# The expert loop of a two-layer block: nine weight places in turn, rows gathered with the selection stationary, and the last turns of the gated units moved

## What is computed

```python
logits = h @ w_router + b_router
topv, idx = lax.top_k(logits, 4)          # of 32 experts
gates = softmax(topv)
# the tokens of an expert, in blocks:
gu = xblk @ w_gate_up[e] + b_gate_up[e]    # 1024 -> 2048
gate = minimum(gu[:, :1024], 7.0); up = clip(gu[:, 1024:], -7.0, 7.0)
act = (up + 1.0) * (gate * sigmoid(1.702 * gate))
y = act @ w_down[e] + b_down[e]            # 1024 -> 1024
out[token] += y * gate_of_token
```

## Time and profile before

| | |
|---|---|
| median of 3 runs | 2026.39 us (2024.31 to 2032.32) |
| the profiled execution | 2024.82 us, of which the span of instructions is 2023.0 us |
| TensorE busy | 1954.4 us (97%), 10632 products |
| VectorE, ScalarE, GpSimd busy | 920.9 us (46%), 534.1 us (26%), 79.8 us (4%) |
| mean granted TensorE clock | 0.992 |
| moved by DMA | 560.29 MB, mean 277 GB/s |
| chain that ended last | PE 64%, DMA 21% (the weights of the experts 20%), DVE 7%, ACT 3% |

### The profile page before, as it was taken

The page is one execution under the profiler, slowest core; times in us unless marked ns, Lnnn a source line. Parts: engine busy times, 40 slices in busy tenths (PEclk is TensorE's granted clock), DMA queues, the critical chain, the costliest instruction groups (busy, mean ns, idle before and its releaser), DMA issues.

```text
span 2023.0 us, 26217 instructions
## 1 busy us (share of the span) xinstructions
PE 1954.4 (97%) x10632; PEld 1235.7 (61%) x10632; DVE 920.9 (46%) x1615; ACT 534.1 (26%) x792; POOL 79.8 (4%) x115
## 2 busy tenths in 40 slices
PE   7989999999999999999999999999999999999998
PEld 5767787444444444344344434687788887878886
DVE  5664556333223332332233233366666545556544
ACT  3444352011011101110010111222434434555432
POOL 1210000000000000000000000010320000000000
PEclk9999999999999999999999999999999999999999
DMA  6342228889999999999999999542326464445452
GB/s 248 137 160 84 94 103 314 365 367 429 427 428 428 428 428 428 428 428 428 427 428 427 429 427 429 212 150 100 105 85 228 151 214 166 158 145 205 170 195 76
DMA packets 106456, 560.29 MB, mean 277 GB/s; under 512 B 5904, under 2 KB 11280, under 8 KB 81808
## 3 DMA queue, kind: packets, MB, share of 16 engines
q1 hardware_dynamic: 102528, 551.61, 67.9%
q10 hardware_dynamic: 3856, 7.67, 1.2%
HBM read 558.21 MB, written 1.05 MB: 276 GB/s over the span
## 4 chain that ended last, share of the span: by engine, by line
PE 64%; DMA 21%; DVE 7%; ACT 3%; issue 2%; POOL 2%; SPq 0%; ACTq 0%; POOLq 0%; DVEq 0%
DMA ring<-in_w_gate_up_dram 20%; PE ps L1101 14%; PE ps L827 9%; PE ps L828 9%; PE ps L829 9%; PE ps L1125 6%; PE ps L1067 3%; PE ps L1200 3%; PE ps L1055 2%; DVE split_w L1997 2%; PE ps L1208 1%; PE ps L887 1%; POOL small L768 1%; PE ps L1325 1%; DMA gains<-in_gains_dram 1%
## 5 line engine op out<-in xcount | busy, mean ns | idle before, releaser
L1101 PE MATMUL ps<-ring,arena 128*64 128x512 f32 x2000 | 440.5, 595 | 8.8 <-DMA ring<-in_w_gate_up_dram 8.8
L1101 PEld LDWEIGHTS ps<-ring,arena 128*64 128x64 f32 x2000 | 139.5, 137 | 294.0 <-issue 269.8
L2373 DVE TENSOR_SCALAR arena<-ps 128x512 f32<-128x512 f32 x32 | 22.1, 692 | 504.6 <-PE ps L1101 504.6
L1956 DVE TENSOR_TENSOR split_w<-ring,split_w 128x1024 fp32r<-128x1024 f32 (+2 forms) x176 | 203.9, 1205 | 77.0 <-ACT split_w L1750 76.5
L1125 PE MATMUL ps<-ring,arena 128*64 128x512 f32 x1024 | 226.8, 595 | 0.0
L827 PE MATMUL ps<-split_w,act_parts 128*128 128x512 f32 (+1 forms) x544 | 209.8, 386 | 2.0 <-issue 1.0
L829 PE MATMUL ps<-split_w,act_parts 128*128 128x512 f32 (+1 forms) x544 | 205.6, 378 | 0.0
L828 PE MATMUL ps<-split_w,act_parts 128*128 128x512 f32 (+1 forms) x544 | 205.3, 377 | 0.0
L1750 ACT ACTIVATE split_w<-ring 128x1024 fp32r<-128x1024 f32 (+2 forms) x176 | 171.7, 1033 | 107.3 <-PE ps L829 107.3
L1125 PEld LDWEIGHTS ps<-ring,arena 128*64 128x64 f32 x1024 | 70.7, 137 | 133.3 <-issue 133.3
L1067 PEld LDWEIGHTS ps<-actT,arena 128*128 128x128 f32 x1056 | 129.9, 200 | 27.5 <-issue 27.5
(11 more groups left out here) (333 smaller groups left out, 2382.2 us busy)
## 6 DMA issues: line engine op xcount, KB each, us to landing
ring<-in_w_gate_up_dram SPq DMA_DIRECT2D x125, 2048.0 KB, 21.9
ring<-in_w_down_dram SPq DMA_DIRECT2D x64, 2048.0 KB, 19.7
ring<-in_f_w_dram SPq DMA_DIRECT2D x28, 2048.0 KB, 8.0
ring<-in_w_in_dram SPq DMA_DIRECT2D x14, 2048.0 KB, 8.0
ring<-in_a_w_in_dram SPq DMA_DIRECT2D x8, 2048.0 KB, 7.9
ring<-in_b_w_qkv_dram SPq DMA_DIRECT2D x6, 2048.0 KB, 7.8
arena<-in_w_gate_up_dram SPq DMA_DIRECT2D x3, 2048.0 KB, 14.0
ring<-in_f_w_dram SPq DMA_DIRECT2D x4, 1536.0 KB, 6.9
```

The costliest lines, as they stand in the source:

```text
L1101: mm = pe.matmul(ps[half, bank, :], xeT[:, 2 * c + j, :], w[:, j, col:col + 512], start=False, stop=(c == 3 and j == 1), skip_group_check= ...
L1956: dve.tensor_tensor(part_place(load, 1, k, n)[:, s_, :], raw_place(load, k, n)[:, s_, :], part_place(load, 0, k, n)[:, s_, :], ALU.subtract)\
L2373: dve.tensor_scalar(gate_c, ps[:, 1, :], 7.0, None, ALU.min).then_inc(m_gate, 1)
```

## The change

Of the expert loop: (1) the six ring places, in the order `RING_ORDER`, and the three extra ones form nine places. In the first 15 blocks (`GROUPED`, written out in groups of three blocks) chunk c of block b goes to place (6b + c) mod 9; from block 15 on the six ring places are used as before. (2) The gather has the selection stationary and the tokens moving: four products of 512 columns, two tiles by two halves of the columns, which land in the lower and the upper 64 partitions of bank 0. The rows are then not turned: ScalarE copies bank 0 to `xe_rows`, four turns of TensorE follow, and VectorE evacuates them as before. (3) The activation's turns go to bank 2, VectorE copies the activation before the rows, and ScalarE copies the rows behind the Silu. (4) The fill of `weightsT` goes from VectorE to GpSimd. Of the gated units: turns 10 and 11 stand in the middle of piece 1's products, one for each tile.

The diff, cut to its core (the renaming of semaphores and unchanged lines are left out):

```diff
@@ -335,20 +335,16 @@
 
 
 EXTRA = 3
-FIRST_SLOTS = (4, 5, 2, 1, 0, 3)
-FIRST_ORDER = (3, 4, 0, 1, 2, 5)
-
-
-def slot_of(b, chunk):
-
-    if b == 0:
-        return FIRST_SLOTS[chunk]
-    return FIRST_SLOTS[(chunk + EXTRA) % RING]
-
-
-def loads_of(b, chunk):
-
-    return loads_before(slot_of(b, chunk)) + (1 if b == 0 or chunk >= EXTRA else 0)
+PLACES = RING + EXTRA
+RING_ORDER = (1, 0, 4, 5, 2, 3)
+GROUP = 3
+GROUPED = 15
+MINBLK = S * TOPK // BLK
+
+
+def place_of(j, chunk):
+
+    return (RING * j + chunk) % PLACES
 
 
 def loads_before(slot):
...
@@ -517,7 +515,9 @@
             return ap
 
         extra = [arena[:, 5120 + SLOT * i:5120 + SLOT * (i + 1)] for i in range(EXTRA)]
+        places = [ring[:, s, :] for s in RING_ORDER] + extra
         h2n = area(0, NT, D)
+        xe_rows = rows[:, 1280:1792]
         gate_c, up_c, sig, act_e = area(2048, 512), area(2560, 512), area(3072, 512), area(17408, 512)
         act_eT, y_e, xeT = area(3584, 4, P), area(4096, 512), area(4608, KD, BLK)
         match, matchw = spot(0, NT * TOPK, BLK), spot(512, NT * TOPK, BLK)
...
@@ -679,36 +679,42 @@
 
                 return w_gu[e, c] if c < 4 else w_dn[e, c - 4]
 
-            def expert_chunk(b, e, c):
-                s = slot_of(b, c)
-                sync.dma_start(ring[:, s, :], expert_weights(e, c)).then_inc(loaded[s], 16)
-
-            for i, c in enumerate(FIRST_ORDER):
-                if i < 2:
-                    sync.wait_ge(pre_split, quarters_done(OUT_LOAD + i, 3))
+            def expert_chunk(place, e, c):
+                sync.dma_start(places[place], expert_weights(e, c)).then_inc(place_in[place], 16)
+
+            def grouped_block(b, j, e):
+
+                for c in range(RING):
+                    if c >= EXTRA:
+                        sync.wait_ge(used[c - EXTRA], b)
+                    elif place_of(j, c) < RING:
+                        sync.wait_ge(used[c + EXTRA], b - 1)
+                    expert_chunk(place_of(j, c), e, c)
+
+            for c in range(RING):
+                if c < 2:
+                    sync.wait_ge(pre_split, quarters_done(OUT_LOAD + c, 3))
                 else:
-                    sync.wait_ge(gemm_ready, G_OUT + i // 2 * 2)
-                expert_chunk(0, 0, c)
+                    sync.wait_ge(gemm_ready, G_OUT + c // 2 * 2)
+                expert_chunk(c, 0, c)
             sync.wait_ge(r_table, 1)
-            blocks = sync.value_load(tab[0:1, 48:49], min_val=TOPK, max_val=MAXBLK)
-            second_e = sync.value_load(tab[0:1, 1:2], min_val=0, max_val=NE - 1)
-            for c in range(EXTRA):
-                sync.dma_start(extra[c], expert_weights(second_e, c)).then_inc(extra_in[c], 16)
-            for c in range(EXTRA, RING):
-                sync.wait_ge(used[c - EXTRA], 1)
-                expert_chunk(1, second_e, c)
-            third_e = sync.value_load(tab[0:1, 2:3], min_val=0, max_val=NE - 1)
-            for c in range(RING):
-                if c < EXTRA:
-                    sync.wait_ge(used[c + EXTRA], 1)
-                else:
-                    sync.wait_ge(used[c], 2)
-                expert_chunk(2, third_e, c)
-            with sync.Fori(3, blocks) as b:
+            blocks = sync.value_load(tab[0:1, 48:49], min_val=MINBLK, max_val=MAXBLK)
+            for b in range(1, GROUP):
+                grouped_block(b, b, sync.value_load(tab[0:1, b:b + 1], min_val=0, max_val=NE - 1))
+            with sync.Fori(GROUP, GROUPED, GROUP) as first:
+                for j in range(GROUP):
+                    e = sync.value_load(tab[0:1, bass.ds(first + j, 1)], min_val=0, max_val=NE - 1)
+                    for c in range(RING):
+                        if c < EXTRA:
+                            sync.wait_ge(used[c + EXTRA], first + (j - 1))
+                        else:
+                            sync.wait_ge(used[c - EXTRA], first + j)
+                        expert_chunk(place_of(j, c), e, c)
+            with sync.Fori(GROUPED, blocks) as b:
                 e = sync.value_load(tab[0:1, bass.ds(b, 1)], min_val=0, max_val=NE - 1)
                 for c in range(RING):
                     sync.wait_ge(used[c], b)
-                    expert_chunk(2, e, c)
+                    expert_chunk(c, e, c)
 
             gdn_out, moba_in, moba_out = (t[n][0].rearrange("(k p) n -> p k n", p=P) for n in
                                           ("a_w_out_2", "b_w_qkv_2", "b_w_out_2"))
...
@@ -777,6 +783,8 @@
                     m += 1
             row_scales(2)
             row_scales(3)
+            pool.wait_ge(r_logits, 2)
+            pool.memset(weightsT, 0.0).then_inc(m_gtsb, 1)
 
             def power(c, n, mult, add, done):
 
...
@@ -1062,28 +1070,43 @@
             def gather(n):
 
                 pe.wait_ge(m_s, n)
-                for k in range(KD):
-                    for tile in range(NT):
-                        mm = pe.matmul(ps[:, 0, k * BLK:(k + 1) * BLK], h2n_c[:, tile, k // 2, k % 2, :],
-                                       sel[:, tile, :], start=(tile == 0), stop=(tile == 1),
-                                       skip_group_check=True)
+                for tile in range(NT):
+                    for h, half in enumerate((low, high)):
+                        mm = pe.matmul(ps[half, 0, :].rearrange("p (c j q) -> p c j q", c=2, j=2),
+                                       sel[:, tile, :],
+                                       h2n_c[:, tile, 2 * h:2 * h + 2], start=(tile == 0),
+                                       stop=(tile == 1), skip_group_check=True)
                 mm.then_inc(m_gathered, 1)
 
+            def turn_rows(n):
+
+                pe.wait_ge(m_row_copy, n)
+                for i in range(4):
+                    mm = pe.transpose(ps[:, 0, i * P:(i + 1) * P], xe_rows[:, i * P:(i + 1) * P],
+                                      ident)
+                mm.then_inc(m_gathered, 1)
+
             pe.wait_ge(r_table, 1)
-            blocks = pe.value_load(tab[0:1, 48:49], min_val=TOPK, max_val=MAXBLK)
+            blocks = pe.value_load(tab[0:1, 48:49], min_val=MINBLK, max_val=MAXBLK)
             gather(1)
+            turn_rows(1)
             pe.wait_ge(bias_split, 1)
 
-            def weights_in(b, at, c):
-
-                if at == 1 and c < EXTRA:
-                    pe.wait_ge(extra_in[c], 16)
-                    return extra[c]
-                s = slot_of(at, c)
-                pe.wait_ge(loaded[s], 16 * b + 16 * loads_of(at, c))
-                return ring[:, s, :]
-
-            def expert_block(b, at):
+            def grouped_weights(g, j, c):
+
+                place = place_of(j, c)
+                lap = (RING * j + c) // PLACES
+                laps = lap + 1 + (loads_before(RING_ORDER[place]) if place < RING else 0)
+                pe.wait_ge(place_in[place], 32 * g + 16 * laps)
+                return places[place]
+
+            def late_weights(b, c):
+
+                laps = loads_before(RING_ORDER[c]) + 2 * GROUPED // GROUP - GROUPED + 1
+                pe.wait_ge(place_in[c], 16 * b + 16 * laps)
+                return places[c]
+
+            def expert_block(b, weights_in):
 
                 pe.wait_ge(m_hot, b + 1)
                 pe.wait_ge(m_gtsb, b + 1)
...
@@ -1093,7 +1116,7 @@
                           skip_group_check=True).then_inc(m_biased, 1)
                 pe.wait_ge(m_xe, b + 1)
                 for c in range(4):
-                    w = weights_in(b, at, c).rearrange("p (j n) -> p j n", n=2 * FF)
+                    w = weights_in(c).rearrange("p (j n) -> p j n", n=2 * FF)
                     for j in range(2):
                         for bank in (1, 2):
...
@@ -1106,11 +1129,11 @@
                 pe.wait_ge(m_y, b + 1)
                 combine((0,))
                 pe.wait_ge(m_act, b + 1)
-                pe.wait_ge(m_xe, b + 2)
                 act_4 = act_e.rearrange("p (q j) -> p j q", j=4)
                 for j in range(4):
-                    mm = pe.transpose(ps[:, 0, j * P:(j + 1) * P], act_4[:, j, :], ident)
+                    mm = pe.transpose(ps[:, 2, j * P:(j + 1) * P], act_4[:, j, :], ident)
                 mm.then_inc(m_turned, 1)
+                turn_rows(b + 2)
                 combine((1,))
                 pe.wait_ge(m_dup, b + 1)
                 for tile in range(NT):
...
@@ -1127,10 +1150,11 @@
                                            w[:, j, n * 512:(n + 1) * 512], start=(c == 4 and j == 0),
                                            stop=(c == 5 and j == 3), skip_group_check=True)
                     mm.then_inc(used[c], 1)
-            for at in range(2):
-                expert_block(at, at)
-            with pe.Fori(2, blocks) as b:
-                expert_block(b, 2)
+            with pe.Fori(0, GROUPED // GROUP) as g:
+                for j in range(GROUP):
+                    expert_block(GROUP * g + j, lambda c: grouped_weights(g, j, c))
+            with pe.Fori(GROUPED, blocks) as b:
```

(47 more changed lines are left out.)

17 lines of the change are left out of this document (9 added, 8 removed).

## The result

| | before | after |
|---|---|---|
| median of 4 runs each | 2027.81 us (2024.31 to 2032.32) | 2006.62 us (2005.11 to 2009.44) |
| the profiled execution | 2024.82 us | 2009.44 us |
| span of it | 2023.0 us | 2007.6 us |
| first request of block 1 to the end of the last down products | 938.56 us | 922.40 us |
| bytes missing between 380 and 430 us, as time at 427.5 GB/s | 14.3 us | 0.1 us |

The ratio is 0.9896, 95% interval 0.9872 to 0.992: about 21 us less, 16 to 26. The forecast was 2007.5 us.

What follows compares the result with a forecast made beforehand. The weights' transfers were taken to bound the expert loop, with one pause. 13.5 (pause) + 1.5 (gather) + 3.9 (gated units) = 18.9 us off 2024.82 gave 2005.9, put at 2007.5 us for the median; range 2002 to 2016.

Steps and rivals of the forecast that it cites:

- What bounds the kernel: Expert loop: weights set the pace, 29.43 us a block; last chunk's landing and TensorE's path behind it set the end.
- the change doesn't close the pause: Rival, expert loop: a request still sits behind a late release; whole pause left, only 5.4 us gained, 2021; chance 0.03.
- Part 1: Expert loop, nine places in turn: the transfers' pause from 396 to 420 us goes entirely, 13.5 us gained.
- Part 2: Expert loop, new gather: TensorE's stretch 1.5 us shorter per block, counting only in the last block, 1.5 us gained.
- Part 3: Start of the loop: block 0 about 1 us earlier, clock at 1.2 GHz; 0 gained, bounds 0 to 3 us lost.
- The release that I feared for: Rival, loop start: block 1's chunk 3 requested up to 2 us late if the clock stays low; 2010; chance 0.06.
- Part 4: Gated units' last turns: both pairs of TensorE's waits on hid_parts go, in two feed-forward layers, 3.9 us gained.
- The clock rival: Expert loop: TensorE's longer waits, 2.3 us a block, let the clock fall; 5 to 10 us lost, about 2013; chance 0.06.
- The slow moving side: Rival, gather: strided moving rows read slowly; twice the time about 2016, chance 0.05; slow enough to lose, 0.04.

Runs made afterwards that it cites:

- changed_again: The changed kernel run once more, unaltered, for comparison in a later group; 2007.61 us, ratio 0.9912 to the kernel before.
- only_gather: Kernel before with only the new gather, its evacuation order and the fill on GpSimd; six ring places kept; 2019.78 us, ratio 0.9974.
- contig: Changed kernel with the gather's moving rows read one after another instead of every second element; 2008.27 us in one run.
- only_places: Kernel before with only the nine places in turn, old gather and gated units kept; 2015.69 us, ratio 0.9953.
- only_places_9: Kernel before with only the nine places, used in the first nine blocks instead of 15; 2021.93 us in one run.
- only_turns: Kernel before with only turns 10 and 11 of the gated units moved into piece 1; 2020.39 us, ratio 0.9972.
- grouped_3: Changed kernel with nine places in the first three blocks only, six from block 3 on; 2009.63 us, ratio 0.9926 to the kernel before.
- combine_early: Changed kernel with both halves of the combination moved ahead of chunk 3's products; 2005.42 us, ratio 0.9901 to the kernel before.
- steady_end: combine_early with a 512-column product that nobody reads on either side of the last combination; 2006.16 us, ratio 0.9904.
- grouped_6: Changed kernel with nine places in the first six blocks only, six from block 6 on; 2008.70 us in one run.
- warm_gather: Kernel before with two 512-column products that nobody reads ahead of the first, old gather; 2031.16 us in one run.

## Why the prediction was right, and where it was not

**What bounds the kernel: right.** The weights' pace is 29.42 us a block after as before. The last chunk's landing and TensorE's path behind it set the end. The rival *the change doesn't close the pause* fell with the first window, 426 GB/s.

**Part 1, 13.5 us for the pause: right for the whole change, too simple for the part.** The pause went entirely; by a window that holds all of it, it was 14.3 us, 0.8 more than the term. But the sentence "After block 14 the loop goes back to six places. That costs nothing" rested on windows at the end of the old loop, where the lead had long been worked off. It holds only since part 2 makes TensorE faster; alone, part 1 pauses for 3.5 us at block 15 and for 1.0 between 380 and 430 us, where "Every request precedes its need" left none, and the part is worth 10.2 us.

**Part 2, 1.5 us: the step that failed is "In 31 of 32 blocks the gain is therefore worth nothing".** It holds while weights are short (from block 10 on in the changed kernel), and not while TensorE lags: there each microsecond brings the release of a place forward. Alone the new gather is worth 8.7 us: 7.1 of pause, of which some 3.0 come from the start (part 3) and the rest from blocks 0 and 1, and 1.6 elsewhere, about the size forecast for the path behind the last chunk. In the sum it didn't show, as part 1 had already taken the same pause; that is how this term could be wrong and the total right. The sizes inside were near: the gather 1.90 us for 1.74, the activation's turns 0.59 and the added ones 0.53 for 0.68 each, the stretch 5.51 for 5.59. TensorE's period, 27.14 in the prediction, is 26.97 us between the first products of blocks 0 and 1. ScalarE's copy is not waited for in the loop, as forecast.

**Part 3, nothing: right in the sum, wrong in its picture.** I had block 0 about 1 us earlier with the clock at 1.2 GHz throughout. Block 0's first product came 355.97 - 349.52 = 6.45 us after block 1's first request instead of 9.41, since the clock came back at 352 to 353 us (6.9 us in changed_again, where it came back at 354.6). The release that I feared for came earlier, not later. "No time is won by it" needs the transfers to run on; in only_gather, where they pause, these 3.0 us are part of the gain.

**Part 4, 3.9 us: right.** Both pairs of waits went, 2.0 us in the first layer by its timeline, and nothing was late behind them.

**Sum.** 18.9 us were forecast: 13.5 + 1.5 in the loop and 3.9 behind it. The loop gave 16.2, about 0.7 us more from the pause and 0.5 from elsewhere in it, and the layers 4.0, so 20.2. The median moved by 21.2 us in the first group and by 16.9 in the second, so that 2006.62 came within 0.9 us of the forecast is partly luck: the terms are confirmed by the loop and the waits, not by the closeness of the medians. The profiled execution shows only 15.4, as some 6.4 us were given back behind the loop; an execution of before isn't free of that either.

**The rivals.** The gather took 1.90 us, far from the 3.2 at which TensorE would set the end. The clock rival is refuted in the loop: with some 2 us of waits in every block the granted clock stayed at 1.00 in all windows from 360 to 1260 us. The slow moving side costs 0.08 us a gather by contig, so the reading without loss that the prediction sets beside this rival is near, but not exact here.

## What to carry to other kernels

Before costing a saving at nothing because another resource sets the mean pace, look at who lags at that time: as long as the consumer is behind the transfers, its speed decides when buffers come free, and each pause of the transfers that it causes is paid in full at the end. A deeper ring is needed only as long as that lead lasts, and the place where the depth is reduced is the next candidate for a pause: here six blocks would have been enough with the fast gather, and fifteen were not with the slow one. Two changes that shorten the same pause must be costed together, and in both orders.

## What the runs showed of the hardware that was not expected

The granted clock at the start of the loop. In the kernel before, after the router's pauses, the granted clock stayed at 1.2 GHz from about 348.5 to about 362 us, through four products of 512 columns and then 32 records of a 128x128 stationary side with 64 moving columns, and rose only some 1.5 us into the products with the weights. TensorE counts as busy from 351 us on. In the three other profiles that have the old gather first in this place (only_places, only_places_9, only_turns) it was the same: the rise came 9.3 to 10.1 us after the gather began. With the new gather, eight records of 512 columns in its place, the rise came 1.6 to 1.7 us after the gather began in only_gather, grouped_3 and the changed kernel, and 2.4 to 3.3 us after it in the five other profiles (changed_again, combine_early, steady_end, contig, grouped_6), so at 352.4 to 355.3 us on the clock and not always at the 352 or 353 that the expectation for warm_gather has. In the three quick ones the clock had fallen at 345.5 to 345.8 us, in the five others at 347.1 to 348.4. With two 512-column products ahead of the old gather it was back at about their end. Why it rose there is not told by these rows. What came with it they do tell: block 0's first product 2.3 to 3.0 us earlier against block 1's first request, of which the gather's own shortness is a part. By itself that moves no end while the transfers run on.

Windows of one microsecond of the kernel before and after; the granted clock is the third number from the end:

```profile
353.00:354.00 1.00, 1.00 (x7) 1.00 (x6) 0.99 (x2) 0.00 (x0) 0.00 (x0) 0.50 0.48 197
...
361.00:362.00 1.00, 1.00 (x4) 0.24 (x2) 0.96 (x3) 0.00 (x0) 0.00 (x0) 0.50 1.11 475
363.00:364.00 1.00, 1.00 (x8) 0.30 (x6) 0.97 (x2) 0.00 (x0) 0.00 (x0) 1.00 1.00 426
```

```profile
351.00:352.00 1.00, 1.00 (x8) 0.38 (x6) 0.99 (x2) 0.00 (x0) 0.00 (x0) 0.50 0.36 102
...
353.00:354.00 1.00, 0.75 (x4) 0.00 (x0) 0.00 (x0) 0.20 (x1) 0.00 (x0) 1.00 0.87 360
```
